# A SwiGLU FFN by seven block products for two of three token groups, the first product's bank emptied by VectorE

## What is computed

```python
    h = rmsnorm(x, g_pre_ffn)
    gate, up = jnp.split(h @ w_ffn_in, 2, axis=-1)
    return x + rmsnorm((jax.nn.silu(gate) * up) @ w_ffn_out, g_post_ffn)
```

## Time and profile before

| what | us |
|---|---|
| median of 3 timed runs (lowest, highest) | 3014.78 (3003.78, 3024.35) |
| profiled execution: first to last instruction (span) | 3010.2 |
| median of the runs less that span | 4.6 |
| PE busy / PE weight loads busy | 2956.3 / 2755.1 |
| DVE / POOL / ACT busy | 1272.8 / 998.7 / 589.5 |

### The profile page before, as it was taken

The page is one execution under the profiler, slowest core; times in us unless marked ns, Lnnn a source line. Parts: engine busy times, 40 slices in busy tenths (PEclk is TensorE's granted clock), DMA queues, the critical chain, the costliest instruction groups (busy, mean ns, idle before and its releaser), DMA issues.

```text
span 3010.2 us, 42170 instructions
## 1 busy us (share of the span) xinstructions
PE 2956.3 (98%) x17729; PEld 2755.1 (92%) x17729; DVE 1272.8 (42%) x1565; ACT 589.5 (20%) x1034; POOL 998.7 (33%) x468
## 2 busy tenths in 40 slices
PE   8999999999999999999999999999999999999998
PEld 8999967788999999999989998676989999999997
DVE  7333345546433223233583334465472232333326
ACT  4222234523000000000241213345130000000003
POOL 2222233233343434333322222422524343333441
PEclk9999989999999999999999999999999999999999
DMA  5222210021111111111122112100301111111111
GB/s 167 40 39 37 34 34 1 1 93 43 42 49 49 42 49 42 48 49 42 33 86 53 30 30 37 31 1 8 114 22 50 49 42 49 49 42 42 42 53 61
DMA packets 200046, 137.16 MB, mean 46 GB/s; under 512 B 38888, under 2 KB 191096, under 8 KB 199424
## 3 DMA queue, kind: packets, MB, share of 16 engines
q1 hardware_dynamic: 187248, 111.01, 13.8%
q10 hardware_dynamic: 12688, 24.59, 2.2%
HBM read 119.64 MB, written 15.94 MB: 45 GB/s over the span
## 4 chain that ended last, share of the span: by engine, by line
PE 74%; issue 12%; DVE 5%; POOLq 5%; ACT 2%; DVEq 1%; POOL 1%; ACTq 0%; DMA 0%
PE acc L623 17%; PE acc L626 17%; PE acc L627 17%; PE acc L1149 5%; PE acc L1152 5%; PE acc L1153 5%; DVE residual L1741 1%; POOLq L547 1%; POOLq L550 1%; PE acc L793 1%; DVE branch L1739 1%; PE acc L775 1%; DVE x_square L1755 1%; DVEq L1740 1%; PE acc L591 1%
## 5 line engine op out<-in xcount | busy, mean ns | idle before, releaser
L623 PE MATMUL acc<-act_hi,slab_hi 128*128 128x352 f32 x2640 | 859.9, 326 | 6.6 <-ACT residual L1393 5.2
L627 PE MATMUL acc<-act_lo,slab_hi 128*128 128x352 f32 x2640 | 846.4, 321 | 0.0
L626 PE MATMUL acc<-act_hi,slab_lo 128*128 128x352 f32 x2640 | 846.1, 321 | 0.0
L451 POOL TENSOR_TENSOR slab_hi<-slab_raw,ones 128x1024 fp32r<-128x1024 f32 x141 | 272.0, 1929 | 993.7 <-PE acc L623 561.5
L623 PEld LDWEIGHTS acc<-act_hi,slab_hi 128*128 128x128 f32 x2640 | 495.2, 188 | 13.3 <-issue 8.6
L626 PEld LDWEIGHTS acc<-act_hi,slab_lo 128*128 128x128 f32 x2640 | 496.7, 188 | 0.0
L627 PEld LDWEIGHTS acc<-act_lo,slab_hi 128*128 128x128 f32 x2640 | 495.0, 187 | 0.0
L2164 DVE TENSOR_TENSOR branch<-acc,branch 128x1056 f32<-128x1056 f32 x160 | 201.1, 1257 | 389.7 <-PE acc L1153 389.7
L453 POOL TENSOR_TENSOR slab_lo<-slab_raw,slab_hi 128x1024 fp32r<-128x1024 f32 x141 | 358.5, 2542 | 21.0 <-issue 0.6
L2154 DVE TENSOR_TENSOR work<-acc,work 128x1056 f32<-128x1056 f32 x44 | 55.2, 1255 | 568.9 <-PE acc L627 568.9
L451 POOL TENSOR_TENSOR small_hi<-slab_raw,ones 128x1024 fp32r<-128x1024 f32 x50 | 95.8, 1917 | 594.4 <-PE acc L623 508.0
(11 more groups left out here) (401 smaller groups left out, 4918.1 us busy)
## 6 DMA issues: line engine op xcount, KB each, us to landing
slab_raw<-in_w_ffn_in SPq DMA_DIRECT2D x88, 512.0 KB, 3.7
slab_raw<-in_w_ffn_out SPq DMA_DIRECT2D x44, 512.0 KB, 3.2
slab_raw<-in_w_in SPq DMA_DIRECT2D x40, 512.0 KB, 3.9
x_spill<-residual ACTq DMA_DIRECT2D x2, 4224.0 KB, 12.6
residual<-x_spill ACTq DMA_DIRECT2D x2, 4224.0 KB, 14.0
slab_raw<-in_w_out SPq DMA_DIRECT2D x16, 512.0 KB, 3.8
out_y_prompt<-out_rows SPq DMA_DIRECT2D x8, 512.0 KB, 3.9
branch<-in_x_prompt ACTq DMA_DIRECT2D x2, 1024.0 KB, 6.5
```

The source lines that it names most:

```text
L451: pool.tensor_tensor(hi, raw, ONES[:, 0:1].broadcast_to([P, SLAB]), ALU.mult)
L623: mm = pe.matmul(out, wh, HH[:, x], start=k == 0, stop=False)
L626: pe.matmul(out, wl, HH[:, x], start=False, stop=False)
L627: mm = pe.matmul(out, wh, HL[:, x], start=False, stop=k == KT - 1)
```

## The change

The first pair, and the gates of the second, are computed as before. Then, for token groups 0 and 1, a pair of weight tiles (2x2 blocks A11, A12, A21, A22, each of 128 rows of output by four k-blocks) times the two groups' activations (B11, B12 over k 0-3 and B21, B22 over k 4-7) is done with seven products in place of eight: P1 = A11 B11, P2 = A12 B21, P3 = S4 B22, P4 = A22 T4, P5 = S1 T1, P6 = S2 T2, P7 = S3 T3, with S3 = A11-A21, S2 = A22-S3, S1 = S2+A11, S4 = A12-S2 and T1 to T4 sums of B blocks. Group 2 keeps its four products. A "wide" is one such block product (12 matmuls) and a "short" the same for the output side (6 matmuls). A gate or up round (`long_round`) has 11 wides. An output product of a pair is two half rounds of 11 blocks (66 matmuls) each. The up round of the second pair stands ahead of the loop. The loop has BODIES = 9 bodies per layer, each a gate round, two half rounds and an up round.

The eight weight combinations of a round are "units". ACT rounds each to hi, POOL subtracts for lo and also makes the sums S1 to S4, in place, in four quarter buffers (QUAD, 128x512 each) that lie over the two raw slots. The finished units live in a ring of 12 places of 256 columns; a unit of a long round takes two. PE's `unit_used` tells when a place is free, POOL's `q_free` when a quarter may be loaded again.

In PSUM, P1 is alone in bank 0 and P2 is later accumulated over it. So the value P1 must be taken out before P2 starts. DVE does this in the gate and up rounds (`chains`, the copy at L2623), and P2's wide waits for it (L1363). The other results are added up by DVE out of banks 2 and 4. DVE also forms the T sums of the FFN's inner activations (`g_t`) and their lo parts (`g_lo_part`, L2649). Semaphores of earlier stages are used again, with offsets, since the new ones would be too many. x is spilled to DRAM (`f_spill`) to make room for T2 to T4, and is brought back after the last up round.

```diff
+                def long_round(r, made, slots, prologue=False):
...
+                    made_by(A21)
...
+                    wide(7, slots[A21], h13, True, False, unit_used)
...
+                        pe.wait_ge(a_out, A_OUT + 2 * (l * ROUNDS + r))
+                    wide(0, slots[A11], h11, True, True, unit_used).then_inc(a_done, 1)
+                    wide(6, slots[A11], h13, True, False)
...
+                    wide(4, slots[S3], h_t3, True, True, unit_used).then_inc(y_done, 1)
...
+                    wide(2, slots[S2], h_t2, True, True, unit_used).then_inc(x_done, 1)
+                    pe.wait_ge(a_out, A_OUT + 2 * (l * ROUNDS + r) + 1)
+                    wide(0, slots[A12], h21, False, True, unit_used).then_inc(a_done, 1)
+                    wide(6, slots[A12], h23, False, True).then_inc(c_done, 1)
...
+                    pe.wait_ge(x_out, X_OUT + 3 * (l * ROUNDS + r) + 1)
+                    wide(2, slots[S1], h_t1, False, True, unit_used).then_inc(x_done, 1)
+                    wide(7, slots[A22], h23, False, True, unit_used).then_inc(c_done, 1)
...
+                    wide(2, slots[S4], h22, False, True).then_inc(x_done, 1)
...
+                    wide(4, slots[A22], h_t4, False, True, unit_used).then_inc(y_done, 1)
...
+                with pe.Fori(0, BODIES) as b:
+                    made = 8 + MADE * b
+                    long_round(1 + 4 * b, made, GATE_SLOTS)
+                    pe.wait_ge(g_ready, G_READY + l * (4 + BODIES) + 4 + b + 1)
+                    half_round(2 + 4 * b, made + 8, OUT_SLOTS[0])
+                    half_round(3 + 4 * b, made + 16, OUT_SLOTS[1])
+                    long_round(4 + 4 * b, made + 24, UP_SLOTS)
...
+                def weave(made, sets, slots, c0=0, c1=BANK, frees=True):
...
+                    lo_unit(made, A21, slots[A21], Q21, c0, c1)
+                    pool.drain()
+                    pool.wait_ge(q_landed[Q11], landed)
+                    pool.tensor_tensor(q21, q11, q21, ALU.subtract).then_inc(unit_sum, 1)
+                    lo_unit(made, A11, slots[A11], Q11, c0, c1)
+                    lo_unit(made, S3, slots[S3], Q21, c0, c1)
+                    pool.drain()
+                    pool.wait_ge(q_landed[Q22], landed)
+                    pool.tensor_tensor(q21, q22, q21, ALU.subtract).then_inc(unit_sum, 1)
+                    lo_unit(made, A12, slots[A12], Q12, c0, c1)
+                    lo_unit(made, S2, slots[S2], Q21, c0, c1)
+                    pool.drain()
+                    pool.tensor_tensor(q11, q21, q11, ALU.add).then_inc(unit_sum, 1)
+                    pool.tensor_tensor(q12, q12, q21, ALU.subtract).then_inc(unit_sum, 1)
...
+                    lo_unit(made, A22, slots[A22], Q22, c0, c1)
...
+                    lo_unit(made, S1, slots[S1], Q11, c0, c1)
...
+                    lo_unit(made, S4, slots[S4], Q12, c0, c1)
...
+                def chains(r, c12, c21, c22, between, behind):
+
+
+                    dve.wait_ge(a_done, A_DONE + 2 * r + 1)
+                    dve.tensor_copy(c12, bank(0, TG)).then_inc(a_out, 1)
+                    dve.drain()
+                    dve.wait_ge(x_done, X_DONE + 3 * r + 1)
+                    dve.tensor_tensor(c21, bank(2, TG), c12, ALU.add).then_inc(x_out, 1)
...
+                def up_round(i, last=False):
...
+                    dve.tensor_tensor(GTF[0][:, :], f(1, 1), f(0, 1), ALU.subtract).then_inc(g_part, 1)
+                    dve.tensor_tensor(GTF[1][:, :], f(1, 1), g12, ALU.subtract).then_inc(g_part, 1)
+                    dve.wait_ge(y_done, Y_DONE + 2 * r + 2)
+                    dve.tensor_tensor(f(1, 0), bank(4, TG), f(1, 0), ALU.add).then_inc(y_out, 1)
...
+                    dve.tensor_tensor(f(1, 0), f(1, 0), unit_of(W2, 1, 0), ALU.mult).then_inc(g_part, 1)
+                    dve.drain()
+                    dve.tensor_tensor(GTF[2][:, :], f(1, 0), GTF[0][:, :], ALU.subtract).then_inc(g_part, 1)
+                    lo(his + 1, 0, 0)
+                    lo(his + 2, 0, 2)
+                    lo(his + 3, 1, 1)
+                    lo(his + 4, 1, 2)
+                    lo(his + 5, 0, 1)
+                    g_lo_part(his + 7, GTL[1][:, :], GTF[1][:, :], GTH[1][:, :])
+                    lo(his + 8, 1, 0)
...
+                    g_lo_part(his + 9, GTL[0][:, :], GTF[0][:, :], GTH[0][:, :])
+                    g_lo_part(his + 9, GTL[2][:, :], GTF[2][:, :], GTH[2][:, :])
+                    dve.drain().then_inc(g_ready, 1)
```

More of the change, by code:

```diff
@@ new lines, in g_part_of, with short @@
+                def g_part_of(j, n):
+                    x = slice(j * T + n * TG, j * T + (n + 1) * TG)
+                    return RH[:, x], RL[:, x]
+                def short(b, units, first, last, gives=None):
+                    for p in range(2):
+                        for i, (slot, (xh, xl)) in enumerate(units):
+                            wh, wl = ring(slot, p * P, (p + 1) * P)
+                            mm = pe.matmul(bank(b + p, TG), wh, xh, start=first and i == 0, stop=False, skip_group_check=True)
+                            if p == i == 0 and gives is not None:
+                                mm.then_inc(gives, 1)
+                            pe.matmul(bank(b + p, TG), wl, xh, start=False, stop=False, skip_group_check=True)
+                            mm = pe.matmul(bank(b + p, TG), wh, xl, start=False, stop=last and i == len(units) - 1, skip_group_check=True)
+                    return mm
@@ L1172, in half @@
-                    def half(m, j):
-                        wh, wl = slab_parts(slots[j][0], m * P, (m + 1) * P)
+                    def half(m, j, gives=None):
+                        slot = LAST_SLOTS[((1, 0), (2, 3))[j][m // 4]]
+                        wh, wl = ring(slot, m % 4 * P, (m % 4 + 1) * P)
                         x = slice(j * T + n * TG, j * T + (n + 1) * TG)
-                        return three(bank((n * KT + m) % 6, TG), wh, wl, RH[:, x], RL[:, x], j == 0, j == 1)
+                        out = bank((n * KT + m) % 6, TG)
+                        mm = pe.matmul(out, wh, RH[:, x], start=j == 0, stop=False)
+                        if gives is not None:
+                            mm.then_inc(gives, 1)
+                        pe.matmul(out, wl, RH[:, x], start=False, stop=False)
+                        return pe.matmul(out, wh, RL[:, x], start=False, stop=j == 1)
@@ new lines, in body @@
+                def body(b, last=False):
+                    gate_round(b)
+                    for unit in range(4):
+                        outs(b, 1, unit)
+                    for unit in range(4, 8):
+                        outs(b, 1, unit)
+                    for unit in range(6):
+                        ups(b, unit)
+                    up_round(b + 1, lambda unit: ups(b, unit), last_outs if last else lambda unit: gates(b + 1, unit), last)
+                t_hi_part(3, TXH[1][:, :], TXF[1][:, :])
@@ new lines, in _ @@
+                t_hi_part(2, TXH[0][:, :], TXF[0][:, :])
+                t_hi_part(1, quarter(HH, 0, 1), by(EP[:, :], 4))
+                t_hi_part(4, TXH[2][:, :], TXF[2][:, :])
+                for unit in range(6):
+                    first_up(unit)
+                up_round(0, first_up, lambda unit: gates(0, unit))
+                with act.Fori(0, BODIES - 1) as b:
+                    body(b)
+                body(BODIES - 1, True)
+                act.wait_ge(y_done, Y_DONE + 2 * (l + 1) * ROUNDS)
```

612 lines of the change are left out of this document (496 added, 116 removed).

## The result

| | median us | runs, lowest to highest |
|---|---|---|
| before | 3016.11 | 4, 3003.78 to 3024.35 |
| after | 3104.93 | 4, 3096.93 to 3111.76 |

The ratio is 1.0304, with a 95% interval of 1.0268 to 1.034: the changed kernel is 3.0% slower. The forecast was 3079 us, 2.1% slower, in a range of 2945 to 3145. The profiled execution has a span of 3110.0 us, against 3010.2 before.

The account below looks back on a forecast made before the run. PE, busy 98% of the span, was taken as the bound. Stalls, clock and half rounds 154.8, ends 16, less 106.6 saved: +64 on 3010.2, plus 4.6 to the median, 3079 us; 8-in-10 range 2945 to 3145.

Parts of the forecast that it names:

- The saving: FFN on PE: 336 fewer matmuls per layer, 672 in all, at 0.1586 us each, 106.6 us less.
- The stall: Gate round's A12 wide: PE waits for DVE's late copy of bank 0, 6.5 us in each gate round.
- The alternation: Up round's tail: DVE and POOL take turns at the SBUF port, 14.3 us from 22.05, ending at U+36.35.
- the bounds of 0 and 9.8: Gate round stall in us: 0 if DVE never waits, 9.8 if each of eleven operations waits for a 512-wide POOL one.
- The clock: Behind the gate round's stall: PE's matmuls run at the low clock, costing 1.5 us each, bounds 0 and 3.1.
- The half round: Second half round: PE waits for POOL's S2 unit, whose ring place frees late, 0.6 us per body.
- The base of a body: One loop body on PE without waits: 396 matmuls, 62.8 us.
- The ends: Each layer's ends: T sums' lo parts 1.3, first-product additions 2.8, last lo parts 2.9, raw loads 1; 8 us per layer.
- The sum: Whole kernel: 154.8 us for 18 bodies plus 16 for ends, less 106.6, +64.
- The harmless port: Up round's tail: DVE's short operations slip between POOL's, or POOL is idle; stall 0, 2935 us; chance 0.21.
- The smaller mechanism: Up round's tail: POOL runs dry after S4, tail ends at 35, low clock falls idle; +6, 3021 us; chance 0.17.
- POOL as the bound: Loop bodies: slow quarter loads and POOL operations make a body about 76 us; +147, 3162 us; chance 0.15.

Follow-up runs that it names:

- the repaired kernel: Changed kernel with the copy of bank 0 and first bank 2 addition moved into the up round's tail, bank 6 short before bank 4's: 2931.62 us, ratio 0.9704.
- the filler: Changed kernel with 24 float32 matmul calls of 128 columns into free bank 1, ahead of PE's wait for the copy in each gate round: 3073.53 us.
- the swap: Half rounds' bank 6 short put ahead of bank 4's, added to the changed kernel with both early DVE operations moved into the tail: 2931.62 us, ratio 0.9704.
- the three SBUF additions: Changed kernel with three unused 352-wide DVE additions, both inputs in SBUF, ahead of the first lo part in up rounds but the last: 3139.57 us.

## Why the prediction held, step by step

**The saving.** 672 fewer matmuls, as counted. Their price of 0.1586 us is borne out: in the repaired kernel 1254 stand in 200 us without waits, 0.1595 each, and of the 106.6 us there come out 85 (the difference of the medians) to 89 (0.0296 x 3016.78) at the end.

**The stall.** 6.5 us were forecast and 6.84 measured, 18 times. The up round starts at 971.47, which is U. The last lo part was to end at U+36.35 = 1007.82 and ends at 1007.86. That it fits to the tenth is in part luck: the eleven operations start at 994.37, U+22.9, where 22.05 had been put, and take 13.5 us in place of 14.3. A step was missing between tail and copy: the copy is the first operation behind the loop's branch on DVE, and the timeline has 0.63 us of "issue" there, where I had counted none. PE in turn stopped at 1002.25, U+30.8 in place of U+30.4, which hides 0.4 of it. The lo parts' mean over both groups is (120 x 1399 + 54 x 784) / 174 = 1208 ns, "near 1.3 us" had been said. The alternation was the right choice between the bounds of 0 and 9.8: the turn takes 1.55 us, and 1.2 + 0.38 had been put. (The bound of 9.8 leaves out the copy's own 0.5, which the forecast of 6.5 has in it; it should have been 10.3.)

**The clock.** This term was too small: 1.5 us, of the one idle stretch in the earlier trace rows, where the filler gives 1.9 and the subtraction 73.33 - 64.35 - 6.84 gives 2.1. The low clock lasted 6.8 us in 14 of 18 gate rounds and 10.2 in 4, where the stretch of the earlier trace rows had 3.4; much of it lies in the idle time, as in the window from 1005.40, where 3.7 of 6.8 us do, and so costs nothing. It stayed within the bound of 3.1.

**The half round.** 0.6 us forecast, 0.67 waited. With the restart of the matmuls it is 64.35 - 63.22 = 1.1 us by the swap, which also took away small waits beside it; I can't part these.

**The base of a body.** 62.8 forecast; 63.2 without any long wait. The sum per body was 62.8 + 6.5 + 1.5 + 0.6 = 71.4 and is 73.3. The missing 1.9 are 0.3 of stall, 0.6 of clock, and 1.0 of base and half round together (64.35 against 62.8 + 0.6).

**The ends.** The span gives 3110.0 - 3010.2 + 106.6 - 18 x (73.33 - 62.8) = 17 us for both layers; 16 had been put. The same sum over the repaired kernel gives 2924.0 - 3010.2 + 106.6 - 18 x 0.4 = 13. Only one of the four parts is seen in a wait of its own, the lo parts ahead of `sum_group`: 2.9 forecast, 2.6 waited. The clock outside the loops differs from run to run by stretches of up to 38 us at 0.50 (outside the gate rounds it is low for 52 us in the changed kernel's profile, for 35 in the one before), so the agreement of the sum is no proof of its parts, and may be luck.

**The sum.** +64 forecast, +100 in the profiled executions; 18 x 1.9 = 34 us of body are nearly the whole difference. The medians of the timed runs differ by 89: the profiled execution lies below its median before and above it after. The 3105 lies in the forecast's own range of 3030 to 3130, but all the terms of a body had been put too small. A price that errs by some tenths at each of four places in a body errs by 1.2% of the time in the end.

**The rivals.** The harmless port would have had lo parts near 0.55 us and bodies of 63 to 64: that is what narrowing POOL's operations gives, and not the kernel itself. The smaller mechanism needed a tail that ends at U+35. POOL as the bound needed bodies of 76 us and waits for L692 in many places; there are 18 of 0.7 us, all in the half round, and one of 1.3 per layer. POOL has 1433 us of 3110, and its loads land in 2.9 us, so the quarters come in time.

## What to carry to other kernels

When two engines share a resource, look not at their busy shares but at what stands behind the contended stretch in the in-order queue, and whether a third engine waits for it. Here all of the contention was harmless but for two short operations that stood behind the tail, and moving these up into the tail, with a swap of two blocks elsewhere, turned 3.0% slower into 3.0% faster. When the first wait is repaired, a second one that it covered comes out: move both, or ask beforehand what is due next behind the same queue.

## What the runs showed of the hardware that was not expected

- The last operation of a loop body and the first of the next, with a drain and the branch between them, stand 0.60 to 0.66 us apart on DVE in the 14 gate rounds that the branch back leads to, and 0.27 to 0.31 in the 4 others, without a wait that the profile shows. (With the three SBUF additions it is 0.49 to 0.65.) For an operation on the critical path this is a reason not to be the first of a body.
- The low clock around an idle stretch of PE of 6.8 us lasts 6.8 or 10.2 us, counted with its share of the idle time. It costs about 2 us, and 5.3 us of filler matmuls inside the stall take it away. The filler is still worth less than taking the stall away.
- In the stretch shown, with both queues full, the two engines alternate, one operation each per 1.55 us. POOL's 512-wide operation, 1.28 us alone, loses some 0.3 by it, and DVE's, 534 ns beside narrow POOL operations, some 1.0. The engine with the short operations pays.
- A float32 matmul call of 128 columns is two matmuls 0.111 us apart in the profile, at a granted clock of 1.00.
